# Gate jobs evicted one iteration earlier, gate stores on the sync queue in 1 KB pieces, and one two-scalar operation per token for the scaled one-hot matrix

## The reference

```python
def peer_ffn(h, w_query, sub_keys, u_tab, v_tab):
    q = (h @ w_query).reshape(B, L, PEER_HEADS, 2, PEER_HALF)
    s = jnp.einsum('blhtd,htnd->blhtn', q, sub_keys)
    s1, i1 = lax.top_k(s[:, :, :, 0], PEER_TOPK)
    s2, i2 = lax.top_k(s[:, :, :, 1], PEER_TOPK)
    ...            # the 16 best of the 256 sums s1 + s2; idx = i1 * 128 + i2
    gate = jax.nn.softmax(top_s, axis=-1)
    ...
    u = u_tab[i_blk]
    a = jax.nn.gelu(jnp.einsum('tkd,td->tk', u, h_blk))
    return jnp.einsum('tk,tkd->td', g_blk * a, v_tab[i_blk])
```

## Time and profile before

| | before |
|---|---|
| median of three runs | 4043.3 us |
| profiled execution | 4064.89 us |
| its span, first to last instruction | 4063.1 us |
| mean granted TensorE clock | 0.943 |
| busy share TensorE, VectorE, ScalarE, GpSimd | 90%, 65%, 35%, 41% |
| expert stage, each layer: first to last gelu | 812.2 and 813.2 us |

### The profile page before, as it was taken

One profiled execution on the slowest core, in us unless ns is written; L12 is line 12 of the kernel. 1 busy time (PEld: TensorE's weight loads), 2 busy tenths in 40 slices (PEclk: granted clock), 3 DMA queues, 4 the chain that ended last, 5 costly groups with the idle time before them and its releaser, 6 DMA issues. The chain is left out here.

```text
span 4063.1 us, 52955 instructions
## 1 busy us (share of the span) xinstructions
PE 3636.7 (90%) x17778; PEld 3158.1 (78%) x17778; DVE 2637.9 (65%) x5262; ACT 1403.6 (35%) x2400; POOL 1658.2 (41%) x1144
## 2 busy tenths in 40 slices
PE   7888999978879779999988899999788887899999
PEld 6467778978879778888873778789788787788887
DVE  7755512867768638888787544148676675388887
ACT  4254433322323223333332543333223232233332
POOL 4623334644646332222156143447455464322221
PEclk8999999988989889999999899999899898999999
DMA  4004225757769589999731132358487686899996
GB/s 138 25 24 136 68 81 174 255 176 235 270 198 310 180 257 389 353 354 354 258 108 33 42 112 65 85 182 276 164 253 247 202 288 196 282 375 354 354 352 245
DMA packets 513025, 858.49 MB, mean 211 GB/s; under 512 B 236577, under 2 KB 340385, under 8 KB 509345
## 3 DMA queue, kind: packets, MB, share of 16 engines
q1 hardware_dynamic: 204064, 486.56, 36.7%
q0 software_dynamic: 73728, 268.47, 17.2%
q10 hardware_dynamic: 235008, 100.69, 9.0%
HBM read 743.37 MB, written 112.20 MB: 211 GB/s over the span
## 5 line engine op out<-in xcount | busy, mean ns | idle before, releaser
L1844 POOL TENSOR_TENSOR t_ul<-t_u,t_uh 128x1024 fp32r<-128x1024 f32 x168 | 405.5, 2414 | 453.7 <-ACT t_uh L1748 453.1
L1857 POOL DMA_INDIRECT t_stages<-in_peer_v,t_idx x256 | 261.3, 1021 | 749.5 <-DVE pair L2048 702.1
L2076 PE MATMUL pair<-h_high,t_uh 128*128 128x384 f32 x1376 | 508.7, 370 | 44.2 <-ACT t_act L1758 24.2
L1758 ACT ACTIVATE t_act<-pair 128x384 f32<-128x384 f32 x256 | 125.8, 491 | 1133.5 <-PE pair L2076 1049.8
L2111 PE MATMUL pair<-t_v_early,t_ah 128*128 128x512 f32 x1536 | 478.2, 393 | 26.8 <-DVE t_v_early L2037 26.8
L2076 PE MATMUL pair<-h_low,t_uh 128*128 128x384 f32 x1376 | 492.8, 358 | 0.0
L2076 PE MATMUL pair<-h_high,t_ul 128*128 128x384 f32 x1376 | 491.3, 357 | 0.0
L2111 PE MATMUL pair<-h_high,t_ah 128*128 128x512 f32 x1536 | 472.8, 389 | 0.0
L2088 PE MATMUL pair<-t_second,t_first 128*128 128x128 f32 x1536 | 232.8, 299 | 181.1 <-ACT t_stages L1780 181.1
L2009 DVE TENSOR_TENSOR t_second<-iota,pair 128x512 f32<-128x512 f32 x192 | 131.9, 687 | 374.0 <-PE pair L2088 337.3
L2088 PEld LDWEIGHTS pair<-t_second,t_first 128*128 128x128 f32 x1536 | 211.4, 207 | 209.9 <-ACT t_stages L1780 209.9
(11 more groups left out here) (425 smaller groups left out, 8216.2 us busy)
## 6 DMA issues: line engine op xcount, KB each, us to landing
t_u<-in_peer_u SPq DMA_DIRECT2D x256, 512.0 KB, 4.3
t_stages<-in_peer_v SPq DMA_DIRECT2D x256, 512.0 KB, 5.3
acts<-t_act ACTq DMA_DIRECT2D x256, 192.0 KB, 4.3
gates<-t_stages ACTq DMA_DIRECT2D x96, 512.0 KB, 7.4
t_stages<-acts SPq DMA_DIRECT2D x256, 192.0 KB, 5.3
t_stages<-gates SPq DMA_DIRECT2D x256, 192.0 KB, 5.6
p_w_raw<-in_peer_wq SPq DMA_DIRECT2D x64, 256.0 KB, 3.0
m_w_raw<-in_w_in SPq DMA_DIRECT2D x48, 256.0 KB, 2.7
```

The costliest lines, as they stand in the source:

```text
L1758: e.activation(act[:, n % A_SLOTS, :], k.bank[n % 2][:, 0:DENSE], ACT.Gelu_apprx_tanh).then_inc(gelu_done, 1)
L1844: e.tensor_tensor(ul[n % U_SLOTS], u[:, n % U_SLOTS, :, :], uh[n % U_SLOTS].bitcast(F32), ALU.subtract).then_inc(u_split, 1)
L1857: e.indirect_dma_start(value_slot[j % V_SLOTS], None, v_rows, bass.IndirectOffsetOnAxis(ap=idx[:, j:j + 1], axis=0)).then_inc(value_got[j ...
L2076: mm = e.matmul(out, a[n % U_SLOTS][:, q, :], b[:, 1:TT, q, :], start=(q == 0 and m == 0), stop=(q == KT - 1 and m == 2))
```

## The change

Five things change, all in `peer_experts`.

The copies of a step's two gate jobs stand ahead of that step's gelu on ScalarE instead of behind it. The gate stores leave ScalarE's queue and stand on SyncE's, at places given by a table (`store_after`) between the loads of expert rows; the scratch tensor is laid out anew, 32 groups of four first keys, so that a store writes pieces of 256 floats, 1 KB. The value stage loads the gates by groups of four steps, 768 KB at once, into two buffers, the second of which is the buffer of the expert rows. And `second` is made by one operation per token (equal to a key, times a gate, both scalars per partition) instead of two operations per four tokens; its keys come from a copy in PSUM, its scalars from a copy of the transposed selection in SBUF.

```diff
+    GROUP = 4
...
+        def store_after(t, half, piece):
+            if half == 0:
+                return START[t] + 13 + piece
+            return START[t] + 21 + (2 * piece if t < TT - 1 else piece // 2)
...
+                def load_gates(turn, g):
+                    at = turn * (BODY // GROUP) + g
+                    e.dma_start(g_store[g % 2], gates[bass.ds(at, 1)].rearrange("o p n -> p (o n)")).then_inc(g_loaded[g % 2], 16)
...
+                    load_act(turn, n)
+                    if n % GROUP == 0 and regroup:
+                        e.wait_ge(gated, at - GROUP)
+                        load_gates(turn, n // GROUP)
...
                     load_u(n)
+                    for t in range(1, TT):
+                        for half in range(2):
+                            for piece in range(PIECES):
+                                if n == store_after(t, half, piece):
+                                    store_gates(t, half, piece)
...
+                    for t in range(1, TT):
+                        for q in range(JOBS):
+                            if START[t] + STEPS * q // KT == n:
+                                evict(t, q)
                     gelu(n)
...
-                        for q in range(JOBS):
-                            if START[t] + (STEPS * (q + 1) - 1) // KT == n:
-                                evict(t, q)
-                                if q >= JOBS // 2 and q % 2 == 1:
-                                    store_gates(t, 0, (q - JOBS // 2) // 2)
-                        piece = n - START[t] - JOBS * STEPS // KT
-                        if 0 <= piece < PIECES:
-                            store_gates(t, 1, piece)
...
-                        e.tensor_tensor(second[:, s, :, :], keys, bcast(selT[1][:, some], 2, NKEY), ALU.is_equal).then_inc(second_ready, 1)
+                        for a in range(SET):
+                            at = SET * q + a
+                            e.tensor_scalar(second[:, s, a, :], iota_all, col[:, 0, at:at + 1], col[:, 1, at:at + 1],
+                                            ALU.is_equal, ALU.mult).then_inc(oh_ready, 1)
                         e.tensor_tensor(first[:, s, :, :], keys, bcast(selT[0][:, some], 2, NKEY), ALU.is_equal).then_inc(oh_ready, 1)
-                        e.wait_ge(second_ready, n + 1)
-                        e.tensor_tensor(second[:, s, :, :], second[:, s, :, :], bcast(selT[2][:, some], 2, NKEY), ALU.mult).then_inc(oh_ready, 1)
```

More of the change, by code:

```diff
@@ L1613, in peer_experts @@
         v = stages[:, 0, 0:half_v].rearrange("p (r d) -> p r d", r=RING)
-        a_in, g_in = (stages[:, 0, half_v + n * RING * SEQ:half_v + (n + 1) * RING * SEQ].rearrange("p (r t) -> p r t", r=RING)[:, :, 0:DENSE]
-                      for n in range(2))
+        a_in = stages[:, 0, half_v:half_v + RING * DENSE].rearrange("p (r t) -> p r t", r=RING)
+        g_store = [stages[:, 0, half_v + RING * DENSE:half_v + (RING + GROUP) * DENSE],
+                   ring[0][:, :, :, :].rearrange("p r k n -> p (r k n)")[:, 0:GROUP * DENSE]]
+        g_in = [store.rearrange("p (s c t) -> p s c t", s=2 * (TT - 1), c=GROUP) for store in g_store]
+        gate_rows = gates.rearrange("g p (s x) -> g p s x", s=2 * (TT - 1))
         with ExitStack() as until_values:
@@ L1723, in _ @@
                     load_u(n)
+                    for t in range(1, TT):
[3 more added lines that the diff above has]
+                                    store_gates(t, half, piece)
+                for piece in range(PIECES):
+                    if store_after(TT - 1, 1, piece) >= NKEY:
+                        store_gates(TT - 1, 1, piece)
                 e.wait_ge(stored[0], 16 * (PIECES - 1) * (TT - 1))
@@ L1735, in _ @@
                 for n in range(RING, BODY):
[L1736 removed]
+                    chunk(0, n, False)
                 with e.Fori(0, TURNS - 1) as turn:
                     for n in range(BODY):
[L1739 removed]
+                        chunk(turn, BODY + n, True)
             @block.scalar
@@ L1762, in gelu @@
                         store_act(n - 1)
[L1764 to L1769, removed]
-                                stage[half][:, some, :]).then_inc(stored[half] if piece else stored_first[half], 16)
                 def evict(t, q):
@@ L2004, in spread @@
                     keys = bcast(k.iota[:, :], 1, SET)
+                    e.tensor_copy(col[:, :, :], k.bank[2][:, P:3 * P].rearrange("p (a t) -> p a t", a=2)).then_inc(step, tl.one())
+                    settle()
                     for q in range(JOBS):
@@ L2268, in scratch_of @@
     return {n: nc.dram_tensor(n, shape, F32).ap() for n, shape in
-            (("scores", (TT, P, 2 * PH, NKEY)), ("gates", (NKEY, NKEY, SEQ - P)), ("acts", (NKEY, P, SEQ - P)), ("memory", (P, KT, MEM)))}
+            (("scores", (TT, P, 2 * PH, NKEY)), ("gates", (NKEY // 4, P, 4 * (SEQ - P))), ("acts", (NKEY, P, SEQ - P)), ("memory", (P, KT, MEM)))}
 def constants():
```

34 lines of the change are left out of this document (22 added, 12 removed).

## The result

The changed kernel takes **3694.9 us** (median of four runs, 3687.7 to 3706.3) against 4040.5 (four runs, 4035.9 to 4045.3): a ratio of **0.9147**, 95% interval 0.9121 to 0.9173. The forecast of 3680 was 15 us too low, and its range of 3650 to 3775 holds the time. The profiled execution of the changed kernel took 3695.5 us, with a span of 3693.7.

The account below looks back on a forecast made before the run. TensorE was held to bound the value stage and to wait for ScalarE's copies in the expert stage. Savings of 317 + 27 + 4 + 18 = 366 us from 4064.9 gave 3699, scaled to 3680; range 3650 to 3775.

Parts of the forecast that it names:

- Copies ahead of the gelu: Expert stage, six windows of gate steps: TensorE no longer waits for ScalarE's copies, 5.95 us a step, 317 us less.
- VectorE hidden: Windows: with the new operation at 0.27 us, VectorE needs 5.2 us a step, under TensorE's 5.95.
- All short operations here scale with their elements: VectorE in the windows: argument against the new operation costing as much as a 512-element one, 0.66 us, 210 us more.
- the limit of 0.37: Windows: highest price in us of the new operation at which VectorE's step, 8x + 3.0, stays under 5.95.
- the first rival: Windows: VectorE is the bound; median 3717 us at 0.40 us an operation, about 3890 at 0.66; chance 0.12.
- Gaps: Four stretches between windows: stores on SyncE no longer hold up ScalarE, 72.7 us each, 27 us less (0 to 35).
- The cover is gone exactly: Gaps: VectorE's routing is ready 75.0 us behind the window's end, TensorE there at 74.9, so late gathered rows show.
- Tail: Last seven expert steps: 30.91 us against a floor of 29.1, so 1.8 a layer, 4 us less in all.
- Start of the value stage: TensorE's idle of 13.2 and 13.7 us a layer falls by 9 each: 18 us less (8 to 24).
- what is left is a gelu, a rounding and two remainders: Where the value stage begins: the idle remaining once gate stores start earlier, 3 to 4 us.
- The slower rival: Value stage: 768 KB gate loads landing late, at 20 us, eat the gain: median 4169 us; chance 0.03.
- The scaling step: Whole kernel: profiled 4064.9 less 366 gives 3699, scaled by 0.9947, median over profiled time, to 3680 us.

Follow-up runs that it names:

- Copies alone: The kernel before, with only the two copies of a step's gate jobs moved ahead of its gelu: 3729.7 us, ratio 0.9205.
- late copies: The changed kernel with the copies put behind the gelu again: 4005.6 us, ratio 0.9896 to the kernel before.
- the ramp in SBUF: The changed kernel, with the 128 numbers that the two-scalar operation compares against read from SBUF instead of PSUM: 3704.3 us, ratio 0.9145.

## Why the prediction was right, and where it was off

**Copies ahead of the gelu: right.** 535.5 us were foretold for six windows, 535.7 measured; less 317, measured 316.8. The clock came back with the waits, from 0.86 to 1.00. The split of the first window's loss into 20 us for the clock and 33 for waiting was off: TensorE was busy for 112.39 of its 142.54 us, so 30.1 us were waits, 15 of 2.01, and 23.1 the slower clock. The sum of the two was right. Copies alone and late copies show that this is the move, and not one of the others.

**VectorE hidden: right, by less room than I held.** I took 0.27 us for the new operation; it is 0.408 long and 0.342 from start to start (262.9 us busy over 768). The term that was mis-sized is the length: my two rows of one-scalar operations gave 0.355 for 128 elements, while the overlap with the next is 0.066, near the 0.08 that I took. "All short operations here scale with their elements" does not hold either: 0.484 us for 256 and 0.743 for 512, 0.408 for 128. A step needs 8 x 0.342 + 3.0 = 5.74 us of VectorE, under TensorE's 5.95; the limit of 0.37 was near, and the first rival with it. Even so the new operation was not what hid VectorE: with the old ones, 1.2 us instead of 1.37 a job, the windows are 89.2 us too. The sentence on the Trainium skill (VectorE: DVE Perf Modes, "The TRN2 errata — SBUF-src ops pay a fixed extra latency per instruction") fares half and half: many small operations did turn out no cheaper than two large ones, while its estimated 0.26 us was too low. That section is about sources in SBUF, and the new operation's lies in PSUM. And here the PSUM source is the dearer, 0.408 against 0.336 us, as its table has it (120 fixed cycles against 58, an estimated 0.065 us).

**Gaps: right, with a slip in the sum.** 27 us were foretold, for the 17 steps of the earlier trace rows. In these the changed kernel takes 70.7 us in every gap, 35.1 less in all; the wait for `t_sel` that I allowed 2 us a gap for falls into the eighteenth step, and over all 18 the gaps gained 25.1. "The cover is gone exactly" is what the trace shows: in three gaps VectorE's `t_sel` is ready 74.8 us behind the window's end, and TensorE is there at 74.9. In the other one it came at 81.6, and TensorE waited:

```profile
2839.27 0.90 PE L2126 MATMUL pair<-ident,t_sel 128*128 128x128 f32 x3 [6.76 <-DVE t_sel L2021]
```

The reason that I gave, late rows, is the smaller part: VectorE waited 2.7 us for one row there, and up to 1.87 in gaps that were in time. The larger part is that some of `route`'s operations on SBUF alone met GpSimd's splits, here beside three of these:

```profile
2778.84 6.48 DVE L1960 TENSOR_TENSOR t_cand<-t_best 128x256 f32<-128x256 f32 x8
2811.22 2.68 DVE L1989 TENSOR_SCALAR t_row<-t_pos 128x128 uint32<-128x128 uint32 x1
2836.91 2.30 DVE L2021 TENSOR_TENSOR t_sel<-t_ex,t_esum 128x128 f32<-128x128 f32 x1
```

```profile
2781.28 2.41 POOL L1868 TENSOR_TENSOR t_ul<-t_u,t_uh 128x1024 fp32r<-128x1024 f32 x1
...
2811.39 2.42 POOL L1868 TENSOR_TENSOR t_ul<-t_u,t_uh 128x1024 fp32r<-128x1024 f32 x1
...
2836.71 2.35 POOL L1868 TENSOR_TENSOR t_ul<-t_u,t_uh 128x1024 fp32r<-128x1024 f32 x1
```

Of VectorE's lines the second takes 0.22 us where GpSimd is idle, and the third 0.29 (in the run with the old one-hot operations). These three and three like them took 14.4 us in this gap and 8.5 to 9.6 in the others, where `t_sel` met a split as well and took 1.9 to 2.0.

**Tail: right** (3.6, foretold 4). **Start of the value stage: too much.** Foretold 18 us less, measured 10. The step that failed is "what is left is a gelu, a rounding and two remainders": I looked at the engines and not at the loads. The idle is as long as before, 9.45 against 8.51 us, now because activation 0 lands only at 1318.4; gone are the stalls of the first chunks. Loading in the order of need moved part of the same idle to between the third chunk and the fourth.

**The small pieces** were named as the cause on ScalarE's queue. Either half of that part is nearly enough for the gaps, which are most of the 30 us beside the copies: 18 steps take 82 to 83 us with neither, 75.7 to 76.1 with larger pieces alone, 75.2 to 77.6 with SyncE's queue alone. At the start of the value stage the halves differ: idle and stage together take 538.2 and 538.1 us with the copies alone, 536.9 and 537.1 with larger pieces on ScalarE's queue, 542.5 and 542.1 with small ones on SyncE's, and 534.7 in the changed kernel.

**The slower rival**, 768 KB loads every fourth step, did not come: they land 8.2 us after their issue, not 18, and TensorE has no gap in the stage after its first chunk. The stretch with 412 GB/s is once more above the 358 that was quoted from the Trainium skill (DMA: Bandwidth & Descriptors, "Specifications"). The slack of 0.7 us a step that this rival was priced with is a step of 4.1 us less VectorE's share; the row beside it, 432.97 of 538.22 over 128, gives 0.82.

**The scaling step.** From the profiled 4064.9 the sum gave 3699, which is 4 us off the profiled 3695.5. That is luck in part: 13.6 us between the two profiles lie in the first two rows of the table, for which the sum has no term, and they make up for the 8 that the value stage gained less than foretold, and for smaller misses. In the medians the change saved 345.7, not the 363 foretold. Of the 20 us by which the sum of 366 was too large there, 8 are the value stage and 2 the gaps; some 6 may be windows, if the 846.2 us in the run with late copies are nearer to an average run of the kernel before than the 852.5 of its profile. The profiled execution of before was 22 us above the median beside it; where that lay in stretches which the change made shorter, a saving read from it is too large, and scaling by 0.9947 took only 2 us off the sum. Where the rest of the 22 us lay stays open. Of the bounds, the lower end counted 10 us more for the ends, where its own range of 8 to 24 around 18 leaves 6.

## What to carry to other kernels

When a matmul waits for a copy out of PSUM, look first at what the copy stands behind in its own engine's order: here the copy was ready to run half a step earlier, and moving it, with no work saved, was worth nine tenths of the gain, since the waits also cost clock. After such a gain look for the engine that now has no room; a part that was meant to relieve it (the new one-hot operation) must be priced by its fixed time per instruction, not by its elements. And where a stage starts, look at the loads that its first step waits for as well as at the instructions; fewer bytes ahead of them brought 2 us a layer at most here.

## What the runs showed of the hardware

While GpSimd's elementwise split ran, VectorE's operations with two inputs in SBUF were held up, and so was its `TENSOR_SCALAR` from SBUF to SBUF; the ones with an operand in PSUM never were. 353 two-scalar operations on PSUM beside a split took 0.408 us in the median and 0.422 at most; with the ramp in SBUF, 151 beside a split took 0.761 in the median and up to 2.49, and 617 others 0.336. Not every operation on SBUF alone is held: 62 `MAX8` of 128 elements beside a split took 0.278 us in the median and 0.284 at most. The Trainium skill (SBUF — State Buffer, "🔬 SBUF: two separate sides") has it as a lock of a port pair that the two engines share, given for a whole instruction, on VectorE's side to operations with two inputs in SBUF or in a mode that uses both ports; the runs agree, down to operations of 0.3 us that end with the 2.4 us split. It goes to whoever starts first, by that section; by these records `t_row` started 0.17 us ahead of its split (2811.22 against 2811.39) and still ended 0.09 us behind it. I had not thought of any of this in the prediction, and it is the larger part of why `t_sel` was late in the one gap.
